# Last feed-forward part: twelve up chunks as seven block products each instead of eight

## The reference

```python
def sq_relu_mlp(h, w1, w2):
    return jnp.square(jax.nn.relu(h @ w1)) @ w2

x = x + g2 * sq_relu_mlp(modulate(x, norm2_g[i], sh2, sc2), mlp_w1[i], mlp_w2[i])
```

## Time and profile before

| | us |
|---|---|
| median of 3 runs | 3146.32 (3144.56 to 3146.48) |
| the profiled execution's own time | 3151.97 |
| its span | 3150.0 |
| PE busy | 3118.6 (99%) |
| DVE busy | 1977.0 (63%) |
| ACT busy | 1228.2 (39%) |
| POOL busy | 615.7 (20%) |

### The profile page before, as it was taken

How to read it: one execution, slowest core, us unless ns; L and a number is a source line. 1 busy time by engine, 2 the same in 40 slices (tenths; PEclk the granted TensorE clock), 3 DMA queues, 4 the chain that set the end, 5 groups by cost and what they waited for, 6 DMA issues and landing times.

```text
span 3150.0 us, 36124 instructions
## 1 busy us (share of the span) xinstructions
PE 3118.6 (99%) x14782; PEld 2536.1 (81%) x14782; DVE 1977.0 (63%) x2664; ACT 1228.2 (39%) x1653; POOL 615.7 (20%) x479
## 2 busy tenths in 40 slices
PE   9999999999999999999999999999999999999998
PEld 7877788888888777888888866788888888888887
DVE  7555666666666457567766657766555589963333
ACT  4234433323432344422235355644433453352222
POOL 1000010000200010499991010012333101010001
PEclk9999999999999999999999999999999999999999
DMA  3222233455222222355533001023332422322221
GB/s 127 84 94 81 81 145 143 150 211 187 94 81 89 82 87 94 104 192 194 190 139 126 27 19 40 15 86 132 114 130 101 160 94 94 108 94 98 103 94 67
DMA packets 55620, 342.38 MB, mean 109 GB/s; under 512 B 5984, under 2 KB 7840, under 8 KB 18208
## 3 DMA queue, kind: packets, MB, share of 16 engines
q1 hardware_dynamic: 54080, 337.46, 29.9%
q10 hardware_dynamic: 1376, 2.62, 0.2%
HBM read 327.47 MB, written 12.58 MB: 108 GB/s over the span
## 4 chain that ended last, share of the span: by engine, by line
PE 79%; POOL 10%; DVE 6%; ACT 2%; issue 2%; DMA 0%; POOLq 0%; ACTq 0%; DVEq 0%
PE PS L264 78%; POOL FA L273 10%; ACT PB L270 1%; PE PS L267 1%; DVE FA L281 1%; DVE PB L273 1%; DVE wl L273 1%; DVE UL L273 1%; DVE PS L273 1%; DVE SC L273 0%; ACT SC L270 0%; DVE UL L281 0%; DVE FA L273 0%; DVE ST L293 0%; ACT FA L270 0%
## 5 line engine op out<-in xcount | busy, mean ns | idle before, releaser
L264 PE MATMUL PS<-UH,wh 128*128 128x512 f32 (+1 forms) x2120 | 837.4, 395 | 2.2 <-DVE wl L273 0.7
L264 PE MATMUL PS<-UH,wl 128*128 128x512 f32 (+1 forms) x2120 | 824.4, 389 | 0.0
L264 PE MATMUL PS<-UL,wh 128*128 128x512 f32 (+1 forms) x2120 | 824.3, 389 | 0.0
L273 DVE TENSOR_TENSOR wl<-raw,wh 128x2048 fp32r<-128x2048 f32 (+2 forms) x255 | 563.0, 2209 | 390.7 <-ACT wh L270 390.6
L264 PE MATMUL PS<-RH,wh 128*128 128x512 f32 (+2 forms) x1640 | 642.9, 392 | 0.9 <-DVE wl L273 0.9
L264 PE MATMUL PS<-RH,wl 128*128 128x512 f32 (+2 forms) x1640 | 637.8, 389 | 0.0
L264 PE MATMUL PS<-RL,wh 128*128 128x512 f32 (+2 forms) x1640 | 637.5, 389 | 0.0
L270 ACT ACTIVATE wh<-raw 128x2048 fp32r<-128x2048 f32 (+2 forms) x255 | 452.7, 1780 | 245.3 <-DMA raw<-in_wall 165.7
L264 PEld LDWEIGHTS PS<-UH,wh 128*128 128x128 f32 x2120 | 400.5, 189 | 105.1 <-issue 17.8
L264 PEld LDWEIGHTS PS<-UL,wh 128*128 128x128 f32 x2120 | 400.7, 189 | 83.4 <-issue 3.8
L264 PEld LDWEIGHTS PS<-UH,wl 128*128 128x128 f32 x2120 | 400.3, 189 | 83.2
(11 more groups left out here) (218 smaller groups left out, 3071.0 us busy)
## 6 DMA issues: line engine op xcount, KB each, us to landing
raw<-in_wall SPq DMA_DIRECT2D x224, 1024.0 KB, 4.8
FA<-in_wmod SPq DMA_DIRECT2D x48, 1024.0 KB, 4.9
raw<-in_wall SPq DMA_DIRECT2D x29, 512.0 KB, 3.6
kspec<-FA SPq DMA_DIRECT2D x8, 1024.0 KB, 6.9
FA<-kspec SPq DMA_DIRECT2D x8, 1024.0 KB, 6.8
PB<-in_window SPq DMA_DIRECT2D x16, 256.0 KB, 4.5
Hs<-in_xT ACTq DMA_DIRECT2D x4, 512.0 KB, 8.0
FA<-in_w SPq DMA_DIRECT2D x4, 512.0 KB, 5.7
```

The lines of the kernel that those rows point to most:

```text
L264: return self.put(self.eng and self.eng.matmul(out, w, x, start=start, stop=stop, skip_group_check=True))
L273: return self.put(self.eng and self.eng.tensor_tensor(out, a, b, op))
```

## The change

In quarters 1 to 3 of M = 3 the twelve up chunks (`SPLIT`) are computed in another way. The 1024 x 256 weights are taken as two-by-two blocks (k halves by halves of the output), the 1024 x 512 input as two-by-two blocks (k halves by halves of the positions), and the four result blocks come from seven products of blocks instead of eight, with sums of blocks as operands. Each product is 4 tiles of k times three matmuls of 256 columns, so a chunk has 84 matmuls of 256 columns in place of 48 of 512.

The sums of input blocks are made once, in quarter 0 (`tile_parts` on POOL: eight adds of 512 columns and four of 1024; ACT and DVE split them in the down chunks of quarter 0). The sums of weight blocks are made for every chunk (`block_sums` on POOL: four adds of 512 columns, reading `raw`), and ACT and DVE split them in two pieces of 1024 (`sums_hi`, `sums_lo`). The quarter of a chunk's own weights that no product uses alone is no longer split. What follows the products changes too: DVE combines them in `SC` (`mix` 0 to 4), and relu, square and high part all run on ACT.

```diff
--- before.py
+++ after.py
...
 WEIGHTS_AT = {5 + 5 * s: s for s in range(4)}
+SPLIT = {("up", 3, 1 + i // 4, i % 4): i for i in range(12)}
...
@@ -772,9 +808,59 @@
                     p.matmul(ps(key), FB[:, HID + 128 * t4:HID + 128 * t4 + 128], w, True, False)
                     p.matmul(ps(key), FB[:, HID + 512 + 128 * t4:HID + 640 + 128 * t4], w, False, True).then_inc("sum", key)
 
+        def seven(tag):
+            _, _, q, j = tag
+            keys = [("s7", q, j, r) for r in range(4)]
+            for r, e in enumerate((("r_11", (q, j)), ("mix", (q, j, 0)), ("mix", (q, j, 3)), ("mix", (q, j, 4)))):
+                take(keys[r], e)
+            def block(r, left, right, start):
+                for k in range(4):
+                    three(ps(keys[r], NC), left(k), right(k), start and k == 0, k == 3)
+            def weights(m, kh):
+                return lambda k: pair(tag, 256 * (4 * kh + k) + 128 * m)
+            def sums(i):
+                return lambda k: tuple(x[:, 128 * k:128 * k + 128] for x in weight_sums(tag, i - 1))
+            def tiles(kh, th):
+                return lambda k: tuple(x[:, 4 * kh + k, NC * th:NC * th + NC] for x in (UH, UL))
+            def tsums(i):
+                return lambda k: tuple(x[:, k, :] for x in tile_sums(i))
+            p.wait_ge("w_lo", tag)
+            block(0, weights(0, 0), tiles(0, 0), True)
+            p.then_inc("sum", keys[0])
+            p.wait_ge("s_lo", (tag, 0))
+            p.wait_ge("t_lo", 2)
+            block(1, sums(2), tsums(2), True)
+            p.then_inc("sum", keys[1])
+            p.wait_ge("s_lo", (tag, 1))
+            p.wait_ge("t_lo", 3)
+            block(2, sums(3), tsums(3), True)
+            p.then_inc("sum", keys[2])
+            p.wait_ge("t_lo", 1)
+            block(3, sums(1), tsums(1), True)
+            p.then_inc("sum", keys[3])
+            p.wait_ge("mix", (q, j, 1))
+            p.wait_ge("t_lo", 4)
+            block(2, weights(1, 1), tsums(4), False)
+            p.then_inc("sum", keys[2] + (1,))
+            p.wait_ge("mix", (q, j, 2))
+            block(3, sums(4), tiles(1, 1), False)
+            p.then_inc("sum", keys[3] + (1,))
+            block(0, weights(0, 1), tiles(1, 0), False)
+            p.then_inc("sum", tag[:3] + (2 * j + 1,))
         def mlp(M, n):
             for q in range(4):
                 for j in range(4):
+                    if ("up", M, q, j) in SPLIT:
+                        seven(("up", M, q, j))
+                        continue
                     ks, first = (2 * j, 2 * j + 1), q == 0 and j == 0
                     keys = [("up", M, q, k) for k in ks]
                     frees = [[("r_x" if M < 2 or first else "r_sq", (M, q, k))] for k in ks]
...
+        def first_copy(tag):
+            _, M, q, j = tag
+            a.wait_ge("sum", ("s7", q, j, 0))
+            if (q, j) > (1, 1):
+                a.wait_ge("mix", (q, j - 2, 4) if j > 1 else (q - 1, j + 2, 4))
+            else:
+                a.wait_ge("r_lo", (M, 0, 7))
+            a.activation(sc(2 + j % 2, 16, 272), ps(("s7", q, j, 0), NC), ACT.Copy).then_inc("m1_c", (q, j))
+        def combined(tag):
+            _, M, q, j = tag
+            x0, x1 = sc(0), sc(1)
+            a.wait_ge("mix", (q, j, 3))
+            a.activation(x1, x1, ACT.Relu)
+            a.settle()
+            a.activation(x1, x1, ACT.Square)
+            a.settle()
+            a.wait_ge("sum", ("dn", M, q - 1, 7))
+            a.activation(hid(M, 2 * j + 1)[0], x1, ACT.Copy).then_inc("r_hi", (M, q, 2 * j + 1))
+            a.wait_ge("mix", (q, j, 4))
+            a.activation(sc(0, 272, 528), sc(0, 272, 528), ACT.Relu)
+            a.wait_ge("sum", ("up", M, q, 2 * j + 1))
+            a.wait_ge("r_lo", (M, q, 2 * j - 2) if j else (M, q - 1, 6))
+            a.activation(sc(0, 16, 272), ps(("s7", q, j, 0), NC), ACT.Relu).then_inc("r_11", (q, j))
+            a.settle()
+            a.activation(x0, x0, ACT.Square)
+            a.settle()
+            a.activation(hid(M, 2 * j)[0], x0, ACT.Copy).then_inc("r_hi", (M, q, 2 * j))
 
...
@@ -1519,7 +1654,13 @@
         def mlp(M, n):
             for q in range(4):
                 for j in range(4):
+                    if ("up", M, q, j) in SPLIT:
+                        first_copy(("up", M, q, j))
                     w_hi(("up", M, q, j), halves_ahead("up", M, q, j))
+                    sums_hi(following(("up", M, q, j)))
+                    if ("up", M, q, j) in SPLIT:
+                        combined(("up", M, q, j))
+                        continue
                     for k in (2 * j, 2 * j + 1):
                         if M < 2:
                             a.wait_ge("r_x", (M, q, k))
...
+        def combined(tag):
+            _, M, q, j = tag
+            u2, u3 = sc(2 + j % 2, 16, 272), sc(2 + j % 2, 272, 528)
+            m6, m7, m5 = (ps(("s7", q, j, r), NC) for r in range(1, 4))
+            v.wait_ge("sum", ("s7", q, j, 1))
+            v.wait_ge("m1_c", (q, j))
+            v.tensor_tensor(u2, u2, m6, ADD).then_inc("mix", (q, j, 0))
+            v.wait_ge("sum", ("s7", q, j, 2))
+            v.settle()
+            v.tensor_tensor(u3, u2, m7, ADD).then_inc("mix", (q, j, 1))
+            sums_lo(following(tag), 0)
+            v.wait_ge("sum", ("s7", q, j, 3))
+            v.wait_ge("mix", (q, j, 1))
+            v.tensor_tensor(sc(1, 272, 528), u3, m5, ADD).then_inc("mix", (q, j, 2))
+            sums_lo(following(tag), 1)
+            v.wait_ge("sum", ("s7", q, j, 2, 1))
+            v.tensor_tensor(sc(1, 16, 272), u2, m7, ADD).then_inc("mix", (q, j, 3))
+            v.wait_ge("sum", ("s7", q, j, 3, 1))
+            v.tensor_tensor(sc(0, 272, 528), u2, m5, ADD).then_inc("mix", (q, j, 4))
+            hidden_low(M, q, 2 * j + 1, sc(1))
+        def hidden_low(M, q, k, x):
+            v.wait_ge("r_hi", (M, q, k))
+            h, lo = hid(M, k)
+            v.tensor_tensor(lo, x, h.bitcast(F32), SUB).then_inc("r_lo", (M, q, k))
...
@@ -2259,6 +2448,11 @@
             for q in range(4):
                 for j in range(4):
                     w_lo(("up", M, q, j), halves_ahead("up", M, q, j))
+                    if ("up", M, q, j) in SPLIT:
+                        if j:
+                            hidden_low(M, q, 2 * j - 2, sc(0))
+                        combined(("up", M, q, j))
+                        continue
                     for k in (2 * j, 2 * j + 1):
                         if M < 2 or (q == 0 and j == 0):
                             s = book.place["relu", M, q, k] = pairs.take(v, ("r_lo", (M, q, k)))
@@ -2290,6 +2484,12 @@
                     gains(8)
                 for j in range(4):
                     w_lo(("dn", M, q, j), halves_ahead("dn", M, q, j))
+                    if j == 0 and ("up", M, q, 3) in SPLIT:
+                        hidden_low(M, q, 6, sc(0))
+                    if M == 3 and q == 0:
+                        tiles_lo((3, 2, 4, 1)[j])
+                    for x in range(2):
+                        sums_lo(following(("dn", M, q, j)), x)
                     for k in (2 * j, 2 * j + 1):
                         v.wait_ge("sum", ("dn", M, q, k))
...
+        def tile_parts():
...
+            g.wait_ge("u_lo", (9, 7))
+            for k in range(8):
+                g.tensor_tensor(fa(BB + 512 * k, 512), UH[:, k, :].bitcast(F32), UL[:, k, :].bitcast(F32), ADD)
+            g.settle()
+            g.tensor_tensor(tile_sums32(3), part(1, 1), part(0, 1), SUB).then_inc("t_sum", 3)
+            g.settle()
+            g.tensor_tensor(tile_sums32(2), tile_sums32(3), part(0, 0), ADD).then_inc("t_sum", 2)
+            g.settle()
+            g.tensor_tensor(tile_sums32(4), part(1, 0), tile_sums32(2), SUB).then_inc("t_sum", 4)
+            g.tensor_tensor(tile_sums32(1), part(0, 1), part(0, 0), SUB).then_inc("t_sum", 1)
+            g.settle()
...
+        def block_sums(tag):
+            w = whole(tag).rearrange("p (k m c) -> p k m c", m=2, c=128)
+            a11, a12, a21, a22 = (w[:, 4 * kh:4 * kh + 4, m, :] for m in range(2) for kh in range(2))
+            s1, s2, s3, s4 = (weight_sums32(tag, i).rearrange("p (k c) -> p k c", c=128) for i in range(4))
+            i = SPLIT[tag]
+            if i >= 2:
+                g.wait_ge("sum", ("up", 3, 1 + (i - 2) // 4, 2 * ((i - 2) % 4) + 1))
+            g.wait_ge("raw%d" % (index[tag] % RAWS), tag)
+            g.tensor_tensor(s1, a21, a22, ADD)
+            g.tensor_tensor(s3, a11, a21, SUB)
+            g.settle()
+            g.tensor_tensor(s2, s1, a11, SUB)
+            g.settle()
+            g.tensor_tensor(s4, a12, s2, SUB).then_inc("s_sum", tag)
...
@@ -3099,6 +3335,8 @@
                 before = plan[r - RAWS]
                 if before[4]:
                     s.wait_ge("w_lo", before[0])
+                    if before[0] in SPLIT:
+                        s.wait_ge("s_sum", before[0])
                 else:
                     s.wait_ge(*before[5])
```

(55 more changed lines are left out.)

26 lines of the change are left out of this document (added).

## The result

The changed kernel takes 3194.0 us (3190.0 to 3195.7), the kernel before 3146.4 on the same chip: a ratio of 1.0148, 95% interval 1.0135 to 1.016. That is 47.6 us more; 51.5 were forecast, and 3198 lies 4 us above the measured time.

What follows compares the result with a forecast made beforehand. PE was taken to bound the kernel (busy 3118.6 of 3150.0 us). Columns -9.6 and chain waits made +30.7; with POOL 7.8 and 5 and clock 8, +51.5 us on the median 3146.3 gave 3198, range 3175 to 3211.

Steps and rivals of the forecast that it cites:

- columns: Twelve up chunks: 84 matmuls of 256 columns take 10.06 us instead of 10.88, saving 9.6 us in all.
- waits in the up chunks, POOL's part with them: Up chunks: PE waits for `mix`; 3.5 (j = 0), 18.0 (middle), 10.1 (j = 3), plus 7.8 us for POOL.
- first down chunks: Start of down chunks, quarters 1 to 3: hidden tile 6 stands behind the next weights, 2.9 us each, 8.7 in all.
- quarter 0's wait: Quarter 0: POOL's `tile_parts` adds hold up DVE's two-input operations before the first down chunk; 5 us, bounds 0 and 7.
- clock, restarts with it: After twelve waits of 2.8 to 4.1 us: eight clock falls of 1 us each, 8 us; bounds 0 and 19.
- the sixth product: Middle up chunks: it waits 0.2 us more, as `sums_lo` stands between `mix` 1 and `mix` 2 on DVE.
- POOL's 1.3 for a middle chunk: Middle up chunks: a DVE subtraction waits for one POOL add; bounds 0.4 and 1.3, 1.3 taken, 7.8 us in all.
- j = 3: Last up chunk: ACT and DVE convert the first down chunk's whole 2048; wait 3.35 us, three times 10.1.
- 0.15 for PE's restart: Up-chunk waits: an allowance for PE refilling, within about 0.19 us to restart.
- The first (no POOL, no clock): Rival: chains as written, POOL and DVE hardly meet, clock stays; +30.7 us, 3177; chance 0.22.
- The second (every wait drops the clock): Rival: clock costs 12 to 19 us instead of 8, quarter 0 pays 7; 3204 to 3211 us; chance 0.18.
- The third (ACT's tail short): Rival: ACT finishes the previous chunk's `combined` before the last product's result; down to 3140 us; chance 0.04.

Runs made afterwards that it cites:

- woven queue: Changed kernel with hidden tile 6 ahead, input sums later, and DVE's up-chunk queue interleaved more finely: 3136.9 us, 0.9967 of the kernel before.
- DVE's order: Changed kernel with DVE's low parts of the next up chunk's weights and pieces of the next sums moved behind `mix` 2: 3164.1 us, 1.0051 of the kernel before.
- ACT and POOL: Changed kernel with ACT's weight high parts one chunk earlier and a POOL constant fill replacing its weight-sum adds: 3145.2 us, 0.9995 of the kernel before.
- tile 6 ahead: Changed kernel with only hidden tile 6's low part moved ahead of the second down chunk's weight low part on DVE: 3186.2 us, 1.0121 of the kernel before.
- sums later: Changed kernel with POOL's input block sums started after quarter 0's last hidden tile, split in its third and fourth down chunks: 3183.8 us, 1.0116 of the kernel before.
- waits filled: Changed kernel with 22, 22 and 16 unused PE matmuls before the fifth product in j = 1, 2, 3: 3183.2 us, 1.0114 of the kernel before.
- the three edits of order: Changed kernel with weights' low part behind `mix` 2, hidden tile 6 ahead, and input sums after quarter 0's up chunks: 3140.5 us, 0.9978 of the kernel before.
- the constant: Changed kernel with POOL filling the weight-block sums with a constant, reading nothing, instead of four adds: 3176.8 us, 1.0093 of the kernel before.

## Why the prediction was right, point by point

| term | forecast, us | by the rows of after | run that shows it |
|---|---|---|---|
| columns | -9.6 | -9.6 (12 x 0.80) | woven queue: 0.9967 |
| waits in the up chunks, POOL's part with them | 39.4 (3.5 + 18.0 + 10.1 + 7.8) | 25.2 (3 x 8.39) | DVE's order; ACT and POOL |
| first down chunks | 8.7 | 8.3 (3 x 2.75) | tile 6 ahead |
| quarter 0's wait | 5 | 4.3 | sums later |
| clock, restarts with it | 8 | 17.4 (8 x 1.6, 3.0, 1.6) | waits filled; sums later |
| sum | 51.5 | 45.6 | |

**Against the measured time.** From the first up matmul of this part to the end of the span the two profiled executions take 358.65 us (2791.35 to 3150.0) and 404.85 (2786.85 to 3191.7): 46.2 more, of which the rows explain 45.6. The spans as a whole differ by 41.7 only, because the execution before came to this part 4.5 us later. So the forecast for the profiled execution, 3203.5, is 10 us above its 3193.5, while the one on the median is 4 above.

**The mechanism** was right in every step but a small one: one chain over ACT's tail, `first_copy`, `w_hi`, `w_lo`, the hidden tile and two adds; POOL's adds on top; the clock behind the waits. The small one is the sixth product: it was to wait 0.2 us for `mix` 2, and in the first up chunk of quarter 1 PE lost 0.04 there. **Two sizes were off**, the waits too long and the clock too cheap. That they cancelled for the most part is luck.

The waits of the up chunks were put at 39.4 and are 25.2. POOL's 1.3 for a middle chunk was near (1.46). The chain was worked out too long: `w_hi` should have ended at 4.83 us of the chunk and ended at 4.07 (2889.84 less 2885.77). The forecast added up the durations of ACT's rows with a hand-over each; in the chain above the two relus take 0.59 us, not 0.79, and `first_copy` and `w_hi` 0.27 and 1.48, not 0.38 and 1.68, as an operation that does not need the result of the one ahead of it starts before that one's record ends, and ACT's tail began 0.2 earlier. In j = 3 the same 0.8 makes 2.5 of 3.35, which is the loss where the clock stays (2.34 and the 0.16 above); the fall in the chunk ahead takes it to 2.06. The 0.15 for PE's restart had no row; the runs show 0.12.

The clock was put at 8, eight falls of 1 us. There were ten: eight in the up chunks and one in quarter 3's down chunks (46.5 us from its start to the final norm's first matmul, 42.2 with the three edits of order: the wait's 2.75 and 1.6 more), each some 1.6 with the restarts, and one of 3.0 in quarter 0. The 1.6 of the earlier trace rows was the right price of a fall taken by itself. The discount for "part of the slow stretch lies in the wait" had no row, but a discount there is: with what the next wait gives back, the eight falls are worth 9.0, not far from the 8. Counted in this way, the waits of the up chunks are 29.3 (3 x 9.75) against 39.4, and the clock is 13.6 (9.0, 3.0, 1.6): what the forecast left out is the two falls outside the up chunks.

**The rivals.** The first (no POOL, no clock) had both mechanisms shown against it, by the constant and by the filled waits. The second (every wait drops the clock) came closer: the clock's cost is in its 12 to 19, though three of the thirteen waits of 1.9 us and over kept the clock, and the chain was shorter. The Trainium skill (TensorE: Matmul & The Clock Gate, HAM oscillation) warns of bursts of matmuls between waits that start cold each time. The trace agrees in part: ten of the thirteen waits cost a fall, but behind eight of the ten PE starts at full clock and falls within 1.5 us, and only behind two is it slow at once. The third (ACT's tail short) did not hold; but the point it named does decide: with total waits under 3.2 us a quarter, as in the woven queue, the change is faster than before.

**Exclusion.** The Trainium skill (SBUF — State Buffer, Who interferes with whom) has a DVE operation with two SBUF inputs and a GpSimd operation that reads SBUF exclude each other for a whole instruction. The runs agree for POOL's two-input adds (1.83 to 3.29), for a fill that reads nothing (POOL's fill lies from 2886.20 to 2888.01, and the hidden tile that DVE began at 2886.43 took its 0.69; the low part came after the fill), and for DVE's adds out of PSUM. They do not for one-input scalings, which read SBUF as well: the hidden tile that began in the first scaling took 0.95, where waiting for that scaling's end (1.28 us away) and then its own 0.69 would make 2.0. The measurement decides.

**What stays open.** Why the clock falls behind one wait and not behind another of the same length.
